# Sparse attention: the gate tiles go to one PSUM bank and the logits take turns in three

## The chip, the cores and the metric

The kernel runs on one core of a Trainium2 chip. The metric is the device time of one execution in microseconds (us); the time before is the median of three executions. The engines are called PE (TensorE), DVE (VectorE), ACT (ScalarE), POOL (GpSimd) and SP (SyncE).

## The reference

The program computes two blocks over 512 tokens of width 1024: a layer of gated linear attention and one of sparse attention, then a hybrid layer of five mixers. The change touches the sparse attention only:

```python
def dsa_mixer(x, cos_h, sin_h, cos_i, sin_i, w_in, w_out):
    ...
    h = x @ w_in                                  # q, k, v, z, indexer parts
    q = apply_partial_rope(h[..., :o1]...)        # 16 heads of 128
    k = apply_partial_rope(h[..., o1:o2]...)      # one key head, shared
    z = h[..., o3:o4]                             # the gate, 16 tiles of 128 columns
    ...
    logits = einsum('bthd,btjd->bthj', q_b, k_sel) * ATTN_SCALE
    probs = softmax(where(valid, logits, -inf))
    o = einsum('bthj,btjd->bthd', probs, v_sel)
    return (o * jax.nn.silu(z)) @ w_out
```

## The kernel before

Everything is written out by hand for each engine, with semaphores between them; there is no scheduler. `phase_dsa` computes the sparse attention feature-major: `qT` (the trace calls it mix_a) holds the queries of 16 heads, `zT` (mix_b) their gates, each head one tile of 128 features x 512 tokens. Selection is a mask: all causal logits are computed and `bias` (the tile `left` in the trace) takes the keys out that the indexer did not choose.

**Tiles.** A query or gate tile is 24 matmuls of 512 columns (8 slices of the width, three products each: high by high, high by low, low by high) into one PSUM bank. PE's `project(n)` makes tile n; tiles 0 to 15 are queries, 16 to 31 gates. Tiles 0 to 21 (`n_early` is 22) are made before the heads; tiles 22 to 31 are made in halves of 12 matmuls between the steps of the heads: both halves of tiles 22, 23, 24, 25 in heads 0, 1, 2, 3, and one half in each of heads 4 to 15 (tile 26 in heads 4 and 5, and so on). A gate tile is freed by two steps: ACT takes tanh of it into `zT` (L1505), DVE multiplies `zT` by the tile (L1592, semaphore `z_gated`). DVE does that for the tile finished in head h after the four masks of head h + 2 and a stream shuffle (L1560, heads 0 to 5 only).

**PSUM.** There are 8 banks. Banks 0 and 1 hold logits (`m % 2`, where m = 4 * head + block), 2 and 3 turned probabilities, 4 and 5 the head's output, 6 and 7 the tiles of `project` (`6 + n % 2`). So tile n waits until tile n - 2 is freed, and logits m wait until logits m - 2 are masked:

```python
if m >= 2:
    pe.wait_ge(sem["masked"], past["masked"] + m - 1)
n = (j + 1) * P
g.product(ps[:, m % 2, 0:n], qT[:, h, j * P:(j + 1) * P], kT[:, 0:n])
```

**One head on PE**, in this order: turn blocks 0 and 1 of the probabilities (L1438), half a gate tile, turn the output of the head before (L1444), turn blocks 2 and 3, in heads 0 to 3 the other half of a tile, `logits(h + 2)`, then the products of head h with v. `logits(h + 2)` is four products of 128, 256, 384 and 512 columns; each is two matmul records (the trace shows `ps<-dsa_kT,mix_a`). The product with v (`ps<-dsa_v,probT`) waits for the copies of the turned probabilities (ACT L1541, DVE L1651) and is 20 records.

**One head on DVE**: reciprocal, copy of block 1 of the turned probabilities (L1651), `gate_out` of the head before (L1664), copy of block 3 (L1651), `mask(h + 2)` (L1636: adds bias to the logits, takes the row's maximum in a second record, and L1639 scales it; the second record raises `masked`), the shuffle, the gate of a tile, and the output's scaling (L1657).

Of the kernel before, what the change touches and what calls it, by code (L numbers as in the profile page):

```python
# [14 lines left out]
P = 128  # L15
T = 512
NT = T // P
D = 1024
KD = D // P
# [15 lines left out]
class Semaphores(dict):  # L35
# [26 lines left out]
    def add(self, name, n):  # L62

        self.count[name] += n
        return n
# [193 lines left out]
def columns(parts, k, cols=slice(None)):  # L259

    return [part[:, k, cols] for part in parts]
# [1016 lines left out]
DSA_HEADS, DH, IDX_HEADS, IDX_DIM, TOPK = 16, 128, 8, 64, 128  # L1278
# [15 lines left out]
def phase_dsa(g, qT, zT, gT, first):  # L1294

    nc, t, ps = g.nc, g.t, g.ps
    sem, past, count, add = g.sem, g.sem.past, g.sem.count, g.sem.add
    IT = IDX_HEADS * IDX_DIM // P
    with ExitStack() as stack:
        kT = g.sb(stack, "dsa_kT", [P, T])  # L1300
# [6 lines left out]
        prob = g.sb(stack, "prob", [P, 2, NT, T])  # L1307
# [7 lines left out]
        bias = left  # L1315
# [7 lines left out]
        PER = CHUNK // P  # L1323
# [3 lines left out]
        n_scores = n_group + 3 * IDX_HEADS // n_group  # L1327
        n_silu = 4
        n_early = DSA_HEADS + n_silu + 2
        late_halves = [(n_early + i // 2, i % 2) for i in range(2 * (n_tiles - n_early))]  # L1330
        two_each = len(late_halves) - DSA_HEADS
        first_half = lambda h: 2 * min(h, two_each) + max(h - two_each, 0)
# [7 lines left out]
        if block:  # L1340

            @block.tensor
            def _(pe):
                w = g.chunk(pe, c_kv)
                tile_ready(pe, 1)
                for j in range(NT):
# [3 lines left out]
                    for k in range(KD):  # L1350
                        ins = g.split_product(ps[:, 1, j * DH:(j + 1) * DH], columns(g.xT, k, slice(j * P, (j + 1) * P)), columns(w, k, slice(DH, 2 * DH)), k == 0, k == KD - 1)
                ins.then_inc(sem["v_tok_ready"], add("v_tok_ready", 1))
                for k in range(KD):
                    ins = g.split_product(ps[:, 0, :], columns(w, k, slice(0, DH)), columns(g.xT, k), k == 0, k == KD - 1)
                ins.then_inc(sem["kT_ready"], add("kT_ready", 1))
                g.release("kT_ready")
                for i in range(IT):
                    if i % PER == 0:
                        w = g.chunk(pe, c_qi + i // PER)
                    for k in range(KD):  # L1360
                        ins = g.split_product(ps[:, 2 + i, :], columns(w, k, slice(i % PER * P, (i % PER + 1) * P)), columns(g.xT, k), k == 0, k == KD - 1)
# [3 lines left out]
                w = g.chunk(pe, c_ki)  # L1365
                for k in range(KD):
                    ins = g.split_product(ps[0:IDX_DIM + IDX_HEADS, 7, :], columns(w, k), columns(g.xT, k), k == 0, k == KD - 1)
# [5 lines left out]
                def project(n, ks=range(KD)):  # L1373

                    if n % PER == 0 and 0 in ks:
                        chunk[0] = g.chunk(pe, c_heads + n // PER)
                    w = chunk[0]
                    if 0 not in ks:
                        pass
                    elif n == 0:  # L1380
                        pass
                    elif n == 1:
                        pe.wait_ge(sem["wi_copied"], past["wi_copied"] + 1)
                    else:
                        b = n - 2
                        done = "q_copied" if b < DSA_HEADS else "z_gated"
                        pe.wait_ge(sem[done], past[done] + b % DSA_HEADS + 1)
                    for k in ks:
                        ins = g.split_product(ps[:, 6 + n % 2, :], columns(w, k, slice(n % PER * P, (n % PER + 1) * P)), columns(g.xT, k), k == 0, k == KD - 1)
                    if KD - 1 not in ks:  # L1390
                        return
                    ins.then_inc(sem["head_ready"], add("head_ready", 1))
                    if n % PER == PER - 1:
                        g.release("head_ready")

                project(0)
                pe.wait_ge(sem["wiT_copied"], past["wiT_copied"] + 1)
                pe.wait_ge(sem["kiT_ready"], past["kiT_ready"] + 2)
                for j in range(NT):
                    ins = nc.tensor.transpose(ps[:, 7, j * IDX_HEADS:(j + 1) * IDX_HEADS], wiT[:, j * P:(j + 1) * P], g.ident[0:IDX_HEADS, 0:IDX_HEADS])  # L1400
                ins.then_inc(sem["wi_ready"], add("wi_ready", 1))
                for n in range(1, 4):
                    project(n)
# [3 lines left out]
                for m, (j, h) in enumerate(pairs):  # L1407
# [3 lines left out]
                    n = (j + 1) * P  # L1411
# [6 lines left out]
                def logits(h):  # L1418
                    pe.wait_ge(sem["q_rotated"], past["q_rotated"] + h + 1)
                    if h == 0:  # L1420
                        pe.wait_ge(sem["kT_rotated"], past["kT_rotated"] + 1)
                        pe.wait_ge(sem["summed"], past["summed"] + len(pairs))
                    for j in range(NT):
                        m = NT * h + j
                        if m >= 2:
                            pe.wait_ge(sem["masked"], past["masked"] + m - 1)
                        n = (j + 1) * P
                        g.product(ps[:, m % 2, 0:n], qT[:, h, j * P:(j + 1) * P], kT[:, 0:n]).then_inc(sem["logits_ready"], add("logits_ready", 1))

                def turn_prob(h, j):  # L1430
                    m = NT * h + j
# [17 lines left out]
                for h in range(DSA_HEADS):  # L1449
# [16 lines left out]
                    for j in range(NT):  # L1466
                        for i in range(j + 1):
                            ins = g.product(ps[:, 4 + h % 2, j * P:(j + 1) * P], probT[:, i, j * P:(j + 1) * P], v[:, i, :], i == 0, i == j)
# [4 lines left out]
            def _(act):  # L1473
# [22 lines left out]
                def project(n):  # L1496
                    h = n % DSA_HEADS
                    act.wait_ge(sem["head_ready"], past["head_ready"] + n + 1)
                    src = ps[:, 6 + n % 2, :]
                    if n < DSA_HEADS:  # L1500
                        nc.scalar.activation(qT[:, h, :], src, ACT.Copy).then_inc(sem["q_copied"], add("q_copied", 1))
                    elif h < n_silu:
                        nc.scalar.activation(zT[:, h, :], src, ACT.Silu).then_inc(sem["z_gated"], add("z_gated", 1))
                    else:
                        nc.scalar.activation(zT[:, h, :], src, ACT.Tanh, scale=0.5).then_inc(sem["z_tanh"], add("z_tanh", 1))  # L1505
                    if n % PER == PER - 1:
                        g.split_high(act, c_heads + n // PER + 1 + RING)
# [3 lines left out]
                for m, (j, h) in enumerate(pairs):  # L1511
                    n = (j + 1) * P
# [22 lines left out]
                for h in range(DSA_HEADS):  # L1535
                    for j in range(0, NT, 2):
                        m = NT * h + j
# [14 lines left out]
            def _(dve):  # L1552
# [35 lines left out]
                def project(n):  # L1588

                    h = n - DSA_HEADS  # L1590
                    dve.wait_ge(sem["z_tanh"], past["z_tanh"] + h - n_silu + 1)
                    nc.vector.scalar_tensor_tensor(out=zT[:, h, :], in0=zT[:, h, :], scalar=1.0, in1=ps[:, 6 + n % 2, :],  # L1592
                                                   op0=ALU.add, op1=ALU.mult).then_inc(sem["z_gated"], add("z_gated", 1))

                for n in range(4):
# [2 lines left out]
                for m, (j, h) in enumerate(pairs):  # L1598
                    n = (j + 1) * P
                    dve.wait_ge(sem["relu"], past["relu"] + m + 1)  # L1600
                    r, w, s = ps[:, score_bank(m), 0:n], wi[:, j, h:h + 1], score[:, j, 0:n]
                    if h == 0:
                        ins = nc.vector.tensor_scalar(s, r, w, None, ALU.mult)
                    else:
                        dve.wait_ge(sem["summed"], past["summed"] + m)
                        ins = nc.vector.scalar_tensor_tensor(out=s, in0=r, scalar=w, in1=s, op0=ALU.mult, op1=ALU.add)
# [11 lines left out]
                for j in score_tiles:  # L1618
                    then(nc.vector.tensor_tensor(score[:, j, j * P:(j + 1) * P], score[:, j, j * P:(j + 1) * P], bias[:, 0, 0:P], ALU.add))
                    n = (j + 1) * P  # L1620
                    for r in range(TOPK // 8):
                        src = (left if r else score)[:, j, 0:n]
# [5 lines left out]
                def mask(h):  # L1628
                    for j in range(NT):
                        m = NT * h + j  # L1630
                        i = m % (2 * NT)
                        n = (j + 1) * P
                        dve.wait_ge(sem["logits_ready"], past["logits_ready"] + m + 1)
                        if h >= 2:
                            dve.wait_ge(sem["prob_turned"], past["prob_turned"] + m - 2 * NT + 1)
                        nc.vector.tensor_tensor_reduce(out=prob[:, h % 2, j, 0:n], in0=ps[:, m % 2, 0:n], in1=bias[:, j, 0:n],  # L1636
                                                                        scale=1.0, scalar=TAKEN, op0=ALU.add, op1=ALU.max, accum_out=peak[:, i:i + 1]).then_inc(sem["masked"], add("masked", 1))
                        dve.wait_ge(sem["masked"], past["masked"] + m + 1)
                        nc.vector.tensor_scalar(shift[:, i:i + 1], peak[:, i:i + 1], -ATTN_SCALE, None, ALU.mult).then_inc(sem["peak_shift"], add("peak_shift", 1))  # L1639
# [1801 lines left out]
def build(nc, t, out, upto=99, dump=None):  # L3441
    g = Program(nc, t, out)
    with g.ctx:
# [84 lines left out]
        with ExitStack() as stack:  # L3528
            mix_at = g.address()
            mix_a, mix_b = (g.sb(stack, f"mix_{n}", [P, KI, T]) for n in "ab")  # L3530

            gT = [g.alias(f"gT_{part}", [P, KI, T], F32R, mix_at + 4 * KI * T * i) for i, part in enumerate(("high", "low"))]
            if upto >= 1:
                phase_gla(g, mix_a, mix_b, gT, gla_first)
            if upto >= 2:
                phase_post(g, 0, gT, post_first[0], False, mix_at)
            if upto >= 3:
                phase_dsa(g, mix_a, mix_b, gT, dsa_first)
            if upto >= 4:
                phase_post(g, 1, gT, post_first[1], True, mix_at)  # L3540
# [30 lines left out]
```

## Time and profile before

| what | value |
|---|---|
| median of 3 executions | 1539.26 us (1538.21 to 1539.73) |
| the profiled execution | 1538.63 us |
| its span on the chip | 1536.7 us |
| PE busy | 1460.2 us, 95% |
| DVE / ACT / POOL busy | 637.6 / 523.9 / 554.4 us |
| mean granted clock of PE | 0.982 |
| heads of the sparse attention | 733 to 889 us from the span's start |

All times in the rows below are microseconds from the start of the span. The profiled execution spends 1.9 us outside its span. A busy PE is not PE at its peak: matmuls are pipelined, one starts long before the record of the one ahead of it ends, so the distance between two starts tells what a matmul costs, and the record's length does not.

### The profile page before, as it was taken

The numbers are of one execution on the slowest core, as the hardware profiler recorded it, in microseconds if no ns is written. First come the engines' busy times: TensorE is split into PE (matmuls) and PEld (weight loads), VectorE is DVE, ScalarE is ACT, GpSimd is POOL, SyncE is SP. The second block draws the span as 40 slices with busy tenths as digits, with TensorE's granted clock in tenths as the row PEclk, the third lists the DMA queues.
The fourth block names the chain that finished last, engine by engine and source line by source line (L and its number), as shares of the span: only waits on it lengthen the run. The fifth ranks groups of instructions, "written<-read, shape, count | busy, mean of one in ns | idle before, by whom it ended". The sixth has DMA issues, their size and how long they took to land. (4 is left out here: it accounts for less than half of the span.)

```text
span 1536.7 us, 25099 instructions
## 1 busy us (share of the span) xinstructions
PE 1460.2 (95%) x10829; PEld 1267.2 (82%) x10829; DVE 637.6 (41%) x1309; ACT 523.9 (34%) x862; POOL 554.4 (36%) x234
## 2 busy tenths in 40 slices
PE   7999999999999999999999999998999999877997
PEld 7898886899997987777777799888988887657886
DVE  6032441133117255389565511634125313576426
ACT  3355223433212322423544421335334224343310
POOL 6423421143332325963462243322434241062212
PEclk9999999999999999999999999999999999988999
DMA  5222220022531322223100053224332220002211
GB/s 169 83 83 83 82 83 28 28 85 86 200 99 67 108 65 88 77 85 108 56 28 29 28 185 104 83 65 148 83 110 84 81 83 28 1 1 74 86 39 55
DMA packets 113756, 121.31 MB, mean 79 GB/s; under 512 B 12529, under 2 KB 107613, under 8 KB 113390
## 3 DMA queue, kind: packets, MB, share of 16 engines
q1 hardware_dynamic: 110096, 113.77, 22.8%
q10 hardware_dynamic: 3550, 5.94, 1.1%
q8 instruction: 85, 1.39, 0.4%
q14 instruction: 25, 0.20, 0.0%
HBM read 113.41 MB, written 6.29 MB: 78 GB/s over the span
## 5 line engine op out<-in xcount | busy, mean ns | idle before, releaser
L196 POOL TENSOR_TENSOR w_low<-w_ring,w_high 128x2048 fp32r<-128x2048 f32 (+2 forms) x94 | 414.8, 4413 | 730.6 <-ACT w_high L184 730.4
L212 PE MATMUL ps<-w_high,xT_high 128*128 128x256 f32 (+1 forms) x1056 | 304.9, 289 | 9.4 <-POOL w_low L454 4.5
L212 PE MATMUL ps<-w_high,xT_low 128*128 128x256 f32 (+1 forms) x1056 | 299.3, 283 | 0.0
L212 PE MATMUL ps<-w_low,xT_high 128*128 128x256 f32 (+1 forms) x1056 | 299.1, 283 | 0.0
L184 ACT ACTIVATE w_high<-w_ring 128x2048 fp32r<-128x2048 f32 (+1 forms) x91 | 171.5, 1885 | 289.8 <-PE ps L212 285.8
L212 PE MATMUL ps<-xT_high,w_high 128*128 128x512 f32 (+1 forms) x600 | 241.2, 402 | 4.0 <-POOL w_low L196 3.0
L212 PE MATMUL ps<-xT_high,w_low 128*128 128x512 f32 (+1 forms) x600 | 238.3, 397 | 0.0
L212 PE MATMUL ps<-xT_low,w_high 128*128 128x512 f32 (+1 forms) x600 | 237.1, 395 | 0.0
L212 PEld LDWEIGHTS ps<-w_high,xT_high 128*128 128x128 f32 x1056 | 202.9, 192 | 17.1 <-issue 7.0
L212 PEld LDWEIGHTS ps<-w_low,xT_high 128*128 128x128 f32 x1056 | 202.8, 192 | 1.7 <-issue 1.7
L212 PEld LDWEIGHTS ps<-w_high,xT_low 128*128 128x128 f32 x1056 | 202.5, 192 | 0.0
L212 PE MATMUL ps<-w_high,gT_high 128*128 128x256 f32 x512 | 145.5, 284 | 3.9 <-DVE gT_low L291 3.9
L212 PE MATMUL ps<-w_high,gT_low 128*128 128x256 f32 x512 | 144.9, 283 | 0.0
L212 PE MATMUL ps<-w_low,gT_high 128*128 128x256 f32 x512 | 144.9, 283 | 0.0
L212 PEld LDWEIGHTS ps<-xT_high,w_high 128*128 128x128 f32 (+1 forms) x600 | 112.3, 187 | 34.2 <-POOL w_low L196 4.0
L212 PEld LDWEIGHTS ps<-xT_high,w_low 128*128 128x128 f32 (+1 forms) x600 | 112.3, 187 | 28.0
L212 PEld LDWEIGHTS ps<-xT_low,w_high 128*128 128x128 f32 (+1 forms) x600 | 112.5, 188 | 26.6
L212 PEld LDWEIGHTS ps<-w_high,gT_high 128*128 128x128 f32 x512 | 98.2, 192 | 4.4 <-DVE gT_low L291 4.4
L212 PEld LDWEIGHTS ps<-w_low,gT_high 128*128 128x128 f32 x512 | 98.3, 192 | 0.0
L212 PEld LDWEIGHTS ps<-w_high,gT_low 128*128 128x128 f32 x512 | 98.2, 192 | 0.0
L1170 DVE SCALAR_TENSOR_TENSOR x<-x,ps 128x512 f32<-128x512 f32 x16 | 10.9, 684 | 102.6 <-PE ps L212 102.6
L1700 POOL TENSOR_TENSOR gT_low<-dsa_gated,gT_high 128x512 fp32r<-128x512 f32 x16 | 20.7, 1294 | 84.7 <-ACT gT_high L1531 84.6
(505 smaller groups left out, 2187.6 us busy)
## 6 DMA issues: line engine op xcount, KB each, us to landing
w_ring<-in_gla_w_in_dram SPq DMA_DIRECT2D x24, 1024.0 KB, 5.3
w_ring<-in_dsa_w_in_dram SPq DMA_DIRECT2D x19, 1024.0 KB, 4.9
w_ring<-in_w_in_dram SPq DMA_DIRECT2D x18, 1024.0 KB, 5.1
w_ring<-in_gla_w_out_dram SPq DMA_DIRECT2D x8, 1024.0 KB, 5.2
w_ring<-in_ple_gate_w_dram SPq DMA_DIRECT2D x8, 1024.0 KB, 5.0
w_ring<-in_dsa_w_out_dram SPq DMA_DIRECT2D x8, 1024.0 KB, 5.1
x_scratch<-x SPq DMA_DIRECT2D x4, 1024.0 KB, 6.7
w_ring<-in_w_out_dram SPq DMA_DIRECT2D x4, 768.0 KB, 4.6
```

The costliest lines, as they stand in the source:

```text
L184: self.nc.scalar.activation(self.slot(self.w_high, i % RING, k, cols), self.slot(self.w_ring, n % RING, k, cols), ACT.Copy).then_inc(self. ...
L196: ins = self.nc.gpsimd.tensor_tensor(low[:, part], whole[:, part], high[:, part].bitcast(F32), ALU.subtract)
L212: return self.nc.tensor.matmul(out, lhs, rhs, start=first, stop=last, skip_group_check=not check)
L1170: nc.vector.scalar_tensor_tensor(out=r[:, j, cols], in0=x[:, j, cols], scalar=ALPHA, in1=ps[:, i, :], op0=ALU.mult, op1=ALU.add).then_inc( ...
L1700: nc.gpsimd.tensor_tensor(gT[1][:, h, :], gated[:, h % 2, :], gT[0][:, h, :].bitcast(F32), ALU.subtract).then_inc(sem["head_low"], add("he ...
```

## The change

The gate tiles from 22 on all use bank 6, so each of them but the first waits for the tile before it instead of the one before that. Bank 7, free after tile 21, becomes a third bank for the logits from head 2 on (m = 8): they go to banks 0, 1 and 7 in turn, and wait for the mask three products back instead of two. Logits m = 8 wait in addition until tile 21 is freed. No instruction is added, removed or moved on any engine: PE, DVE, ACT, POOL and SP execute the same rows in the same order, and what differs is the bank that some rows name and the value that some of PE's waits ask for.

```diff
+        tile_bank = lambda n: 6 + n % 2 if n < n_early else 6
+        third = 2 * NT
+        logit_bank = lambda m: (0, 1, 7)[m % 3] if m >= third else m % 2
...
                     else:
-                        b = n - 2
+                        b = n - 1 if n > n_early else n - 2
                         done = "q_copied" if b < DSA_HEADS else "z_gated"
                         pe.wait_ge(sem[done], past[done] + b % DSA_HEADS + 1)
                     for k in ks:
-                        ins = g.split_product(ps[:, 6 + n % 2, :], ...)
+                        ins = g.split_product(ps[:, tile_bank(n), :], ...)
...
                         m = NT * h + j
+                        if m == third:
+                            pe.wait_ge(sem["z_gated"], past["z_gated"] + n_early - DSA_HEADS)
                         if m >= 2:
-                            pe.wait_ge(sem["masked"], past["masked"] + m - 1)
+                            pe.wait_ge(sem["masked"], past["masked"] + (m - 2 if m > third else m - 1))
                         n = (j + 1) * P
-                        g.product(ps[:, m % 2, 0:n], ...)
+                        g.product(ps[:, logit_bank(m), 0:n], ...)
```

ACT's tanh and DVE's gate read `tile_bank(n)`, and DVE's mask reads `logit_bank(m)`.

## Rows read from the trace of the kernel before

**Rows 1.** Waits of all engines in 725 to 892: who waited for whom, total, times, longest.
```profile
PEld ps L212 <- DVE peak L1636: 15.1, 33, 0.7
```

**Rows 2.** Waits of PE in 725 to 892.
```profile
PE ps L212 <- DVE peak L1636: 4.1, 12, 0.4
PE ps L212 <- ACT probT L1541: 1.7, 2, 0.8
```

**Rows 3.** Busy time in stretches: nine heads, then two stretches after the attention.
```profile
784.37:868.28 83.91, 80.92 (x488) 65.04 (x487) 48.33 (x162) 39.81 (x106) 34.21 (x21) 1.00 0.12 39
...
1053.00:1060.00 7.00, 5.01 (x24) 4.92 (x25) 6.49 (x14) 4.97 (x14) 0.00 (x0) 0.51 0.40 150
...
1193.00:1197.00 4.00, 4.00 (x24) 4.00 (x23) 3.97 (x6) 0.00 (x0) 0.00 (x0) 0.57 0.17 60
```

**Rows 4.** Timeline of PE, logits(8) in head 6: start, length, tile, records.
```profile
803.02 0.28 PE L212 MATMUL ps<-dsa_kT,mix_a 128*128 128x128 f32 x1
803.24 0.60 PE L212 MATMUL ps<-dsa_kT,mix_a 128*128 128x256 f32 x2
804.17 0.59 PE L212 MATMUL ps<-dsa_kT,mix_a 128*128 128x384 f32 x1 [0.33 <-DVE peak L1636]
804.60 0.91 PE L212 MATMUL ps<-dsa_kT,mix_a 128*128 128x384 f32 x2
804.92 1.02 PE L212 MATMUL ps<-dsa_kT,mix_a 128*128 128x512 f32 x2
805.35 0.59 PE L212 MATMUL ps<-dsa_kT,mix_a 128*128 128x512 f32 x1
805.78 0.27 PE L212 MATMUL ps<-dsa_v,probT 128*128 128x128 f32 x1
```

**Rows 5.** Timeline of DVE around the same logits.
```profile
803.22 0.69 DVE L1651 COPY probT<-ps 128x512 f32<-128x512 f32 x1
803.83 0.28 DVE L1636 CUSTOM_DVE_ANT_0 prob<-ps,left 128x128 f32<-128x128 f32 x1
804.03 0.08 DVE L1636 DVE_READ_ACCUMULATOR2_ANT peak<- 128x1 f32 x1
```

**Rows 6.** Timeline of PE, logits(2) in head 0.
```profile
740.21 0.27 PE L212 MATMUL ps<-dsa_kT,mix_a 128*128 128x128 f32 x1
740.99 0.91 PE L212 MATMUL ps<-dsa_kT,mix_a 128*128 128x384 f32 x2
742.60 0.27 PE L212 MATMUL ps<-dsa_v,probT 128*128 128x128 f32 x1
```

**Rows 7.** Timeline: the gates of tiles 21 and 22, and PE's first weight load of tile 23.
```profile
734.53 0.68 DVE L1592 SCALAR_TENSOR_TENSOR mix_b<-mix_b,ps 128x512 f32<-128x512 f32 x1
740.41 0.60 ACT L1505 ACTIVATE mix_b<-ps 128x512 f32<-128x512 f32 x1 [2.75 <-PE ps L212]
744.28 0.66 DVE L1592 SCALAR_TENSOR_TENSOR mix_b<-mix_b,ps 128x512 f32<-128x512 f32 x1
745.05 0.19 PEld L212 LDWEIGHTS ps<-xT_high,w_high 128*128 128x128 f32 x1
```

**Rows 8.** Timeline: masks, shuffle and gate of tile 26 in head 5, load of tile 27.
```profile
795.79 0.56 DVE L1636 CUSTOM_DVE_ANT_0 prob<-ps,left 128x384 f32<-128x384 f32 x1 [0.23 <-PE ps L212]
796.65 0.69 DVE L1636 CUSTOM_DVE_ANT_0 prob<-ps,left 128x512 f32<-128x512 f32 x1
798.12 0.66 DVE L1592 SCALAR_TENSOR_TENSOR mix_b<-mix_b,ps 128x512 f32<-128x512 f32 x1
798.90 0.19 PEld L212 LDWEIGHTS ps<-xT_high,w_high 128*128 128x128 f32 x1
```

**Rows 9.** Timeline: gate of tile 27 in head 7, load of tile 28.
```profile
816.11 0.68 DVE L1592 SCALAR_TENSOR_TENSOR mix_b<-mix_b,ps 128x512 f32<-128x512 f32 x1
817.55 0.19 PEld L212 LDWEIGHTS ps<-xT_high,w_high 128*128 128x128 f32 x1
```

More of the change, by code:

```diff
@@ L1388, in project @@
                     for k in ks:
-                        ins = g.split_product(ps[:, 6 + n % 2, :], columns(w, k, slice(n % PER * P, (n % PER + 1) * P)), columns(g.xT, k), k == 0, k == KD - 1)
+                        ins = g.split_product(ps[:, tile_bank(n), :], columns(w, k, slice(n % PER * P, (n % PER + 1) * P)), columns(g.xT, k), k == 0, k == KD - 1)
                     if KD - 1 not in ks:
@@ L1424, in logits @@
                         m = NT * h + j
+                        if m == third:
+                            pe.wait_ge(sem["z_gated"], past["z_gated"] + n_early - DSA_HEADS)
                         if m >= 2:
-                            pe.wait_ge(sem["masked"], past["masked"] + m - 1)
+                            pe.wait_ge(sem["masked"], past["masked"] + (m - 2 if m > third else m - 1))
                         n = (j + 1) * P
-                        g.product(ps[:, m % 2, 0:n], qT[:, h, j * P:(j + 1) * P], kT[:, 0:n]).then_inc(sem["logits_ready"], add("logits_ready", 1))
+                        g.product(ps[:, logit_bank(m), 0:n], qT[:, h, j * P:(j + 1) * P], kT[:, 0:n]).then_inc(sem["logits_ready"], add("logits_ready", 1))
                 def turn_prob(h, j):
@@ L1498, in project @@
                     act.wait_ge(sem["head_ready"], past["head_ready"] + n + 1)
-                    src = ps[:, 6 + n % 2, :]
+                    src = ps[:, tile_bank(n), :]
                     if n < DSA_HEADS:
@@ L1591, in project @@
                     dve.wait_ge(sem["z_tanh"], past["z_tanh"] + h - n_silu + 1)
-                    nc.vector.scalar_tensor_tensor(out=zT[:, h, :], in0=zT[:, h, :], scalar=1.0, in1=ps[:, 6 + n % 2, :],
+                    nc.vector.scalar_tensor_tensor(out=zT[:, h, :], in0=zT[:, h, :], scalar=1.0, in1=ps[:, tile_bank(n), :],
                                                    op0=ALU.add, op1=ALU.mult).then_inc(sem["z_gated"], add("z_gated", 1))
@@ L1635, in mask @@
                             dve.wait_ge(sem["prob_turned"], past["prob_turned"] + m - 2 * NT + 1)
-                        nc.vector.tensor_tensor_reduce(out=prob[:, h % 2, j, 0:n], in0=ps[:, m % 2, 0:n], in1=bias[:, j, 0:n],
+                        nc.vector.tensor_tensor_reduce(out=prob[:, h % 2, j, 0:n], in0=ps[:, logit_bank(m), 0:n], in1=bias[:, j, 0:n],
                                                                         scale=1.0, scalar=TAKEN, op0=ALU.add, op1=ALU.max, accum_out=peak[:, i:i + 1]).then_inc(sem["masked"], add("masked", 1))
```

## The prediction

> **What bounds the kernel now.** I read first who waits for whom in the stage that is touched, then the stage's busy times, then the timeline of one head. In 725 to 892 the records of PE show 4.1 us of idle time before products of L212 that the masks of L1636 release, in 12 places, and 1.7 us for the copies of the turned probabilities [rows 2]. The weight loads ahead of the same products wait 15.1 us in 33 places for the same masks [rows 1]. So PE waits for the logits' banks, and the question is how long. From 784.37 (logits(6)) to 868.28 (logits(15)) lie nine heads, 9.32 us each; PE is busy 80.92 of 83.91 us, DVE only 48.33, 5.4 us a head, and ACT 39.81 [rows 3]. PE sets the pace of this stage, at full granted clock (1.00), and a microsecond taken from its wait is a microsecond of the program as long as nothing takes the wait's place.
>
> The timeline of logits(8) shows the wait [rows 4]. The products start at 803.02 (128 columns), 803.24 (256), 804.17 (384) and 804.92 (512), and the product with v at 805.78: 2.76 us. What they would need without a wait comes from starts that nothing holds up: two records of 128 columns from 803.02 to 803.24, 0.11 us each; 256 columns, twice that, 0.22; 384 columns from 804.60 to 804.92, 0.32; 512 columns from 804.92 to 805.35, 0.43. Twice each is 2.16 us. The difference is **0.60 us**: 384 columns could have started at 803.68 (803.24 + 0.44) and started at 804.17, and their first record kept the array 0.43 instead of 0.32, since the weights for the second weren't loaded ahead. The 512 columns lose nothing: 804.60 + 0.32 is 804.92.
>
> Why it waits: bank m % 2 of the third block is that of the first block, and DVE's mask of that starts at 803.83, when the copy of the turned block (803.22, 0.69 long) is nearly through; the maximum is out at 804.11, and PE goes on at 804.17, 0.06 later [rows 4, 5]. In heads 0 to 3 a half tile lies between the turns and the logits, so the copy is long done; there the same stretch is 740.21 to 742.60, 2.39 us, and 0.23 are lost [rows 6].
>
> **The change, part by part.** *Third bank for the logits.* 14 heads (0 to 13) make logits with m of 8 or more. The third block now waits for a mask of the head before, long done, and the fourth for the first block's mask. In the ten heads 4 to 13 that mask releases at 804.17 in the times of [rows 4], where the fourth block's weights would be wanted at 803.68 + 0.32 = 804.00 and its first column at 804.32; a load needs the 0.11 by which loads and starts of 128 columns follow each other, so 804.28 is in time. Gain: 10 x 0.60 = 6.0 us. In heads 0 to 3 it is 4 x 0.23 = 0.9 us. Together 6.9 us. Next in PE's queue is the product with v, which waits for DVE's copy: it ends at 803.91 and the product comes to 805.18, 1.2 us to spare [rows 4, 5]. Heads 14 and 15 have no logits in between, and the 1.7 us there [rows 2] stay.
>
> *The extra wait of m = 8* for tile 21: its gate ends at 735.21, logits(2) start at 740.21 [rows 6, 7]. Cost 0; without this cover it would hold PE with everything behind it in its queue.
>
> *One bank for the gates.* Nine tiles (23 to 31) now wait for the tile just before. What stands behind this wait on PE is the half tile, the turns of blocks 2 and 3, and with them DVE's copies and ACT's. The release is DVE's gate, queued behind four masks and a shuffle. Tile 22's is through at 744.94, 0.06 more for the release, and PE wants the weights of tile 23 at 745.05: 0.05 us to spare [rows 7]. Both ends come 0.23 earlier after the change, since in these heads the masks of blocks 3 and 4 wait for PE's logits themselves; so tile 23 is a tie, and tiles 24 to 26, whose gates and loads repeat this pattern, are too; I take 0.1 us for the four together. Tile 27 (made from head 6 on) is not quite: PE wants it at 798.90 now and 0.60 earlier, 798.30, then. DVE gains less: the 0.23 that block 3's mask idled, and 0.14 since the mask of 384 columns takes 0.56 + 0.16 (the 0.16 is what lies beyond the record between 803.83 and 804.27, 0.44 for a mask of 0.28) where 0.86 went by from 795.79 to 796.65. So the gate ends at 798.78 - 0.37 = 798.41 and releases at 798.47: **0.17 us late** [rows 5, 8]. Tiles 28 to 31 have no shuffle before them: the gate is through at 816.79 now, 816.42 then, and wanted at 817.55 - 0.60 = 816.95 [rows 9]. Cost of this part 0.1 + 0.17, about 0.3 us; the bound from above, if each of the nine came late by a whole mask of 0.69 [rows 8], is 6.2 us.
>
> The DMAs, POOL's work and everything behind the attention are released by these engines, and come earlier by the same time.
>
> **Sum.** 6.9 - 0.3 = 6.6 us. The profiled execution, 1538.63 us with a span of 1536.7, would take 1532.0; the median of the three is 0.63 above it, so I predict 1539.26 - 6.6 = **1532.7 us**. The lower bound of the gain is what the records show as idle. With 4.1 us, less the waits of logits(0) and (1), which stay, it is about ten times the 0.33 of [rows 4], 3.3 us, less 0.3: 1536.3. I take the distances between starts, because the records of 256 columns run to 803.84 (803.24 + 0.60), 0.16 us after the next start could have come at 803.68 [rows 4], so idle between records misses that much at each wait.
>
> On this choice the Trainium skill ("Perfetto Trace Analysis", Identifying the Most-Contended Engine) has a rule: matmul busy time is a bad measure, since matmuls are pipelined. By the busy time the sum is 3.0 us of gain, by the starts 6.6.
>
> **Rivals.** *A: the gates bind.* A single bank makes each tile's start wait for its predecessor's whole evacuation. For it: five of nine starts have no more than 0.05 us to spare. Against it: between two tiles lie the logits, v and two turns, and the gate is through in that time. If DVE is one mask (0.69) later than I reckon at the five tight starts, 3.5 us are lost and 3.1 are left: 1536.2. Chance 0.08. *A as a loss, the other side:* with evacuation fully exposed, ACT 0.60 and DVE 0.66 [rows 7], nine starts cost 11.3 us, and the program ends 4.4 slower, 1543.7. It decides against the change from 0.77 us per start (6.9 / 9) and shows as slower than the bound below from 1.1. Chance 0.03.
>
> The Trainium skill says as much ("Perfetto Trace Analysis", Matmuls): independent matmul groups should rotate through banks, so that one's evacuation overlaps the next's matmuls. It speaks for the logits' part and against the gates'; in the trace the next gate tile does not follow at once, so I give it little.
>
> *B: the wait only moves.* If the first block's mask came later after the change, the fourth block would wait in place of the third. For it: that mask follows the copy of a block that PE has just turned. Against it: that copy's time hangs on PE alone, and DVE has 9.32 - 5.4 us of slack a head. The idle records alone would then be won, 3.0: 1536.3. Chance 0.07. *C: the granted clock elsewhere.* The stages after come earlier by 6.6 us and may meet the low clock otherwise: in 1193 to 1197 PE worked all the 4.0 us at 0.57, which cost 1.7 [rows 3]. One such stretch more or less is 1.7 us, two 3.4. This widens the range both ways and is no case of its own, but at a chance of 0.03 it takes 4 us or more of the gain.
>
> **Chances and range.** My forecast 0.79, A 0.08, B 0.07, C 0.03, A as a loss 0.03. A measurement of this kernel tells about 0.2%, 3.1 us, from no change. Faster by more (under 1536.2): my forecast and half of A, B and C, 0.88. Within it: 0.09. Slower by more: 0.03. The range: below, the full 6.9 and one stretch of low clock less, 1530.7; above, where A and B lie, 1536.3.
>
> **What would show it.** In the profile after: the waits of PE's products for L1636 fall from 4.1 us to the 0.7 of the first two heads or so; heads 4 to 13 take 8.72 us instead of 9.32, with 2.16 from the first logits to the product with v; a new wait of PE for L1592 is seen at tile 27, under 0.2 us, and perhaps at 23 to 26; PE's copies and DVE's order stay. I am wrong if PE waits for L1592 at nine tiles by 0.7 us or more each, if the wait for L1636 stands before the fourth block with 0.5 us, or if the heads gain 6 us and the stages after 1053 give them back.

## The result, and the profile after

| | before | after |
|---|---|---|
| median of six executions each, taken in turns | 1538.85 us | 1531.0 us (1528.66 to 1532.64) |
| ratio, 95% interval | | 0.9947 (0.9936 to 0.9959) |
| profiled execution, span | 1538.63, 1536.7 us | 1532.64, 1530.9 us |
| the kernel again, five executions (run e1) | 1538.18 us | 1531.74 us, ratio 0.9954 (0.9942 to 0.9965) |

By the ratio the kernel is faster by 0.53%, 8.2 us of 1538.85, on the first measurement and by 0.46%, 7.1 us, on the second; the first pair of medians differs by 7.85 us, the second by 6.44. Forecast were 6.6 us. The page of the kernel after, its first two lines:

```profile
span 1530.9 us, 25099 instructions
...
PE 1458.2 (95%) x10829; PEld 1269.7 (83%) x10829; DVE 636.9 (42%) x1309; ACT 522.6 (34%) x862; POOL 554.2 (36%) x234
```

The waits of PE in 725 to 892, kernel after; it answers to [rows 2] (the lines of the file moved by 5, so L1641 is the mask that was L1636):

```profile
PE ps L212 <- ACT probT L1546: 1.7, 2, 0.8
PE ps L1449 <- DVE kiT L1662: 0.8, 1, 0.8
PE ps L212 <- DVE peak L1641: 0.7, 2, 0.4
```

Of the twelve waits for the masks two are left, those of the first two heads. The weight loads of PE still wait for the masks in 15 places, 5.3 us in all instead of 15.1 [rows 1], but that costs nothing, as the timeline of logits(8) shows. First PE, then its weight loads, then DVE; start, length, tile, records:

```profile
801.80 0.28 PE L212 MATMUL ps<-dsa_kT,mix_a 128*128 128x128 f32 x1
...
802.46 0.81 PE L212 MATMUL ps<-dsa_kT,mix_a 128*128 128x384 f32 x2
802.78 0.91 PE L212 MATMUL ps<-dsa_kT,mix_a 128*128 128x384 f32 x2
803.10 1.02 PE L212 MATMUL ps<-dsa_kT,mix_a 128*128 128x512 f32 x2
803.53 0.59 PE L212 MATMUL ps<-dsa_kT,mix_a 128*128 128x512 f32 x1
803.96 0.27 PE L212 MATMUL ps<-dsa_v,probT 128*128 128x128 f32 x1
...
802.95 0.34 PEld L212 LDWEIGHTS ps<-dsa_kT,mix_a 128*128 128x128 f32 x2 [0.30 <-DVE peak L1641]
...
802.00 0.69 DVE L1656 COPY probT<-ps 128x512 f32<-128x512 f32 x1
802.61 0.28 DVE L1641 CUSTOM_DVE_ANT_0 prob<-ps,left 128x128 f32<-128x128 f32 x1
802.82 0.08 DVE L1641 DVE_READ_ACCUMULATOR2_ANT peak<- 128x1 f32 x1
```

From 801.80 to 803.96 lie 2.16 us, where 2.76 lay in [rows 4]. The 384 columns start 0.66 after the first product, and both their records take 0.32. The load that waits is now that of the fourth block: it is let go at 802.95, 0.05 after the maximum of the first block is out (802.82 + 0.08), and the 512 columns start at 803.10, the 0.32 after 802.78 that they would have needed anyway. The wait is there and costs nothing.

Busy time of nine heads, logits(6) to logits(15), kernel after (PE, PEld, DVE, ACT, POOL, granted clock, DMA share, GB/s):

```profile
784.21:862.84 78.63, 78.63 (x488) 65.70 (x487) 47.59 (x162) 38.79 (x106) 34.41 (x21) 1.00 0.12 41
```

It answers to the first of [rows 3]: 8.74 us a head instead of 9.32, and PE has no idle time left.

The gates: DVE's gate of tile 22 and the first load of tile 23, then the gate of tile 26 in head 5, PE's turn and the load of tile 27 (timeline, kernel after), for [rows 7, 8]:

```profile
744.79 0.66 DVE L1597 SCALAR_TENSOR_TENSOR mix_b<-mix_b,ps 128x512 f32<-128x512 f32 x1
...
745.56 0.19 PEld L212 LDWEIGHTS ps<-xT_high,w_high 128*128 128x128 f32 x1
...
796.99 0.66 DVE L1597 SCALAR_TENSOR_TENSOR mix_b<-mix_b,ps 128x512 f32<-128x512 f32 x1
...
797.34 0.49 PE L1443 MATMUL ps<-ident,prob 128*128 128x128 f32 x3
...
797.70 0.19 PEld L212 LDWEIGHTS ps<-xT_high,w_high 128*128 128x128 f32 x1
```

Tile 23 is loaded 0.11 after the gate ends, as before the change: no wait. Tile 27 is loaded at 797.70, 0.05 after its gate, and its matmuls start 0.36 after the turn where the other heads show 0.25: 0.11 us lost.

Last, the whole attention, from the first product of logits(2) to the first of the output projection, and what comes behind it. Kernel before, then kernel after:

```profile
740.21:889.90 149.69, 143.93 (x863) 116.57 (x862) 82.82 (x266) 68.30 (x172) 60.26 (x38) 1.00 0.09 29
889.90:1536.70 646.80, 598.84 (x5467) 534.53 (x5465) 257.39 (x506) 207.50 (x342) 200.27 (x73) 0.97 0.24 78
```
```profile
740.95:883.85 142.90, 140.46 (x863) 117.72 (x862) 82.00 (x266) 67.16 (x172) 60.20 (x38) 1.00 0.09 30
883.85:1530.90 647.05, 599.04 (x5467) 534.71 (x5465) 257.33 (x506) 207.46 (x342) 200.29 (x73) 0.97 0.24 78
```

The attention is 6.79 us shorter (149.69 - 142.90). The part ahead of it took 0.74 us more in this execution and the part behind 0.25 more, so the spans differ by 5.8. The medians differ by 7.85. What lies between these three numbers is the question that the experiments had to answer.

### The profile page after: what moved, and what is told of

Read it like the earlier page. It is cut to its first block and busy times, and to the rows that moved or that the text cites. A ratio compares the mean times of both kernels' runs of the same rounds, so it can differ in the third digit from the quotient of the medians.

```text
span 1530.9 us, 25099 instructions
## 1 busy us (share of the span) xinstructions
PE 1458.2 (95%) x10829; PEld 1269.7 (83%) x10829; DVE 636.9 (42%) x1309; ACT 522.6 (34%) x862; POOL 554.2 (36%) x234
## 5 line engine op out<-in xcount | busy, mean ns | idle before, releaser
L196 POOL TENSOR_TENSOR w_low<-w_ring,w_high 128x2048 fp32r<-128x2048 f32 (+2 forms) x94 | 414.8, 4414 | 731.8 <-ACT w_high L184 731.6
L212 PE MATMUL ps<-w_high,mix_high 128*128 128x256 f32 (+1 forms) x144 | 45.3, 315 | 6.3 <-DVE late L3313 3.9
```

The lines of the kernel that those rows point to most:

```text
L196: ins = self.nc.gpsimd.tensor_tensor(low[:, part], whole[:, part], high[:, part].bitcast(F32), ALU.subtract)
L212: return self.nc.tensor.matmul(out, lhs, rhs, start=first, stop=last, skip_group_check=not check)
```

## The experiments

**Theory.** The change takes 6.8 us out of the attention, in every execution, by the wait for the masks alone; the rest of the difference is low granted clock elsewhere (the clock of PE that the profile shows as granted, 1.00 for full), which moves from execution to execution. **Rivals.** The change gains 8 us, a part outside the attention; the banks and not the waits make the gain; a single bank for the gates costs much that something else pays for.

### The same two kernels again (e1, e2)

No edit: the kernel after, and the kernel before.

> The changed kernel itself once more, to see what varies. Theory: the attention gains 6.8 us by the trace (first logits of head 0 to the last turn), always; what the median gained beyond that, 8.2 us in all against 6.6 forecast, is the low granted clock before and behind the attention, which falls in other places and lengths from execution to execution. Then the new ratio lies nearer 0.9956 (6.8 us) than 0.9947, single runs spread over 3 us or more again, and the profile shows the attention's length equal to that of the first profile within 0.1 us while the stretches of low clock outside it differ. Rival: the change gains 8 us in every execution, 1.4 of it outside the attention; then the ratio is 0.9947 again and the parts outside the attention are shorter than before by 1.4 us at like clock.

> The kernel before once more, nothing changed: what no change looks like. Ratio 1.000 within 0.1%; the attention as long as in the first profile of before within 0.1 us. If single runs differ by 3 us here too, the spread is not the change's. By the theory the stretches of low clock outside the attention move; by the rival (a gain of 8 us in every execution) they stay.

Measured: e1 1531.74 us, ratio 0.9954 (0.9942 to 0.9965), single executions 1529.52 to 1533.01; e2 1538.71 us, ratio 1.0001 (0.9993 to 1.001), single executions 1536.03 to 1540.33. The kernel before spreads over 4 us as well. Windows of e2, attention and behind:

```profile
741.83:891.65 149.82, 144.03 (x863) 116.59 (x862) 82.76 (x266) 68.27 (x172) 60.19 (x38) 1.00 0.09 29
891.65:1536.10 644.45, 600.37 (x5467) 535.09 (x5465) 257.57 (x506) 207.72 (x342) 200.55 (x73) 0.97 0.24 78
```

The same program, and behind the attention it took 644.45 us where the first profile has 646.80; the attention is the same within 0.13. The part that the change doesn't touch varies by 2.4 us between these two executions of one kernel. The ratio of e1 lies at the 0.9956 that 6.8 us would give, and the part behind the attention (647.05 us in the first profile of the kernel after, 646.79 in e1) is within 0.3 us of the first profile of before and longer than in e2, so the rival that 1.4 us are gained there every time finds no support. The two ratios themselves can't tell 6.8 us from 8: their intervals overlap.

### One half of the change, and its banks without its wait (e3, e4)

e3 keeps the gates' single bank and takes the third bank for the logits back; e4 keeps both edits of the banks, but lets PE wait for the mask two products back again:

```diff
 # e3
-        logit_bank = lambda m: (0, 1, 7)[m % 3] if m >= third else m % 2
+        logit_bank = lambda m: m % 2
 # e3 and e4
-                            pe.wait_ge(sem["masked"], past["masked"] + (m - 2 if m > third else m - 1))
+                            pe.wait_ge(sem["masked"], past["masked"] + m - 1)
```

> Half of the change: the gate tiles from 22 on in bank 6 alone, the logits in banks 0 and 1 as before (bank 7 idle, the extra wait for tile 21 kept). Theory: in the old pace every gate is released 0.05 us before PE wants the next tile's weights, so this costs 0 to 0.3 us: ratio 1.000, no or hardly any wait of PE for L1592, waits for the masks 4.1 us as before. Rival (a single bank exposes the evacuation at each of nine starts): a wait at each, 3 us or more, ratio 1.002 or above.

> The change with the logits in three banks, but waiting for the mask two products back as before. Nothing is left out of the computation. Theory: the gain is the wait's alone, so it vanishes: the waits for the masks are 4.1 us again, the heads take 9.32 us, ratio 1.000. Rival (other banks are faster in themselves, by less interference of DVE's reads and PE's writes): a part of the gain stays, at least 1 us.

Measured: e3 1538.35 us, ratio 1.0 (0.9992 to 1.0009); e4 1538.94 us, ratio 1.0001 (0.9992 to 1.0011). Both show 4.1 us in 12 waits of PE for the masks. The attention by the same marks (first e3, then e4) is as long as the 149.69 and 149.82 us of the kernel before, and so are nine heads of e4, logits(6) to logits(15):

```profile
741.80:891.57 149.77, 143.99 (x863) 116.60 (x862) 82.76 (x266) 68.28 (x172) 60.21 (x38) 1.00 0.09 29
```
```profile
742.05:891.79 149.74, 143.96 (x863) 116.59 (x862) 82.76 (x266) 68.28 (x172) 60.14 (x38) 1.00 0.09 29
...
786.19:870.12 83.93, 80.93 (x488) 65.05 (x487) 48.29 (x162) 39.81 (x106) 34.20 (x21) 1.00 0.12 39
```

So a single bank for the gates costs nothing in the old pace, and three banks gain nothing as long as PE waits for the same mask: the gain is the wait's.

### How near the single bank is to its edge (e5, e6)

DVE's gate of a tile goes behind `scale_out`, which waits for the product with v: in e5 on the kernel after (one bank), in e6 on the kernel before (two). The last `gate_out` then waits for the last gate.

```diff
-                    for n in late_done(h):
-                        project(n)
                     scale_out(h)
+                    for n in late_done(h):
+                        project(n)
...
+                dve.wait_ge(sem["z_gated"], past["z_gated"] + DSA_HEADS)
                 gate_out(DSA_HEADS - 1)
```

> The changed kernel with DVE's gate of a tile put behind the scaling of the head's output, which waits for the product with v. Theory: with one bank each of the nine tile starts waits for that gate. The scaling starts about when PE has ended the product, 0.20 us after the first turn; 0.69 for it, 0.66 for the gate and 0.06 for the release make the gate 1.3 to 1.4 us later than PE wants the weights: 9 x 1.36 = 12.2 us more than the changed kernel, 5.4 more than before, ratio 1.0035. Rival (the single bank has slack that I do not see): under 5 us more than the changed kernel, ratio under 0.999.

> The kernel before, two banks for the tiles, with the same late gate. Theory: a tile waits for the tile two before it, so the late gate costs nothing: ratio 1.000, no wait of PE for L1592, waits for the masks 4.1 us. Rival: the late gate is itself the cost (it pushes back DVE's next copy, which PE's turns wait for), and then this kernel is slower too, by 3 us or more.

Measured: e5 1545.27 us, ratio 1.0046 (1.0032 to 1.0059); e6 1538.58 us, ratio 0.9994 (0.9983 to 1.0004), with 4.0 us of waits for the masks and none for a gate. PE's waits in e5, and one of the nine starts (tile 28 in head 8), timeline:

```profile
PE ps L212 <- DVE mix_b L1597: 9.8, 9, 1.1
...
821.70 0.69 DVE L1662 TENSOR_TENSOR kiT<-ps,inv_total 128x512 f32<-128x512 f32 x1 [1.14 <-PE ps L212]
822.31 0.68 DVE L1597 SCALAR_TENSOR_TENSOR mix_b<-mix_b,ps 128x512 f32<-128x512 f32 x1
...
823.13 0.47 PE L212 MATMUL ps<-xT_high,w_high 128*128 128x512 f32 x1 [1.14 <-DVE mix_b L1597]
```

The gate ends at 822.99, and PE starts the tile at 823.13, after a turn at 821.50: 1.63 us, where 0.25 is usual. The attention takes 154.9 us by the same marks, 12.0 more than with the gate in its place, 1.33 for each of the nine starts; 12.2 were expected. With one bank the late gate costs 12 us, and with two banks nothing (the attention of e6 takes 149.68 us). So a single bank can cost more than the third bank gains, once its release comes late; in the kernel after, the gate is just early enough.

### The waits that are left (e7, e8)

In heads 14 and 15 no logits cover the copies of the turned probabilities, and PE waits 1.7 us for ACT [rows 2]. In e7 the half tile of these heads is cut in two: a quarter tile stays before `turn_out`, the other quarter goes behind the turns of blocks 2 and 3, where it covers the copies. DVE's gate goes ahead of the shuffle. e8 also lets POOL make the low half of head 15 before the split of the weights.

```diff
                     for n, half in halves_of(h)[:1]:
-                        project(n, half_tiles[half])
+                        ks = half_tiles[half]
+                        project(n, ks[:2] if last_two else ks)
                     if h:
                         turn_out(h - 1)
                     turn_prob(h, 2)
                     turn_prob(h, 3)
+                    for n, half in halves_of(h)[:1]:
+                        if last_two:
+                            project(n, half_tiles[half][2:])
...
-                    if n_scores + h < DSA_HEADS:
-                        swap_query(n_scores + h)
                     for n in late_done(h):
                         project(n)
+                    if n_scores + h < DSA_HEADS:
+                        swap_query(n_scores + h)
```

> The changed kernel, improved in two places: the gate ahead of the shuffle (frees tile 26 in time for tile 27, 0.11 us), and in heads 14 and 15, which have no logits to cover the copies of the turned probabilities, only a quarter of the half tile before the turn of blocks 2 and 3 and the rest behind it. Theory: the two waits of PE for L1541, 0.83 us each in the records and about 1.0 from start to start, go: the attention takes 140.8 us instead of 142.9 and the program 2 us less, ratio 0.994. Rival: tile 31 is ready later, ACT's and POOL's splits of the next weights start later, and POOL's low half of head 15, behind them, holds PE at the start of the output projection: the attention is shorter, the stage after it longer, and little or nothing of the 2 us stays.

> As the one before, and POOL makes the low half of head 15 ahead of the split of the weights. Theory: if the rival of the run before holds, this one gives the 2 us back: PE does not wait for POOL at the start of the output projection, ratio 0.994. Rival: the split of the weights then comes too late for PE at the second chunk of the projection, with a wait for L196 of up to 4.6 us.

Measured: e7 1529.68 us, ratio 0.9942 (0.9928 to 0.9955); e8 1529.51 us, ratio 0.9942 (0.993 to 0.9955). The attention of e7, and the end of head 14 on PE, where the quarter tile runs from the turns to the product with v without a gap:

```profile
741.39:882.00 140.61, 139.83 (x863) 117.64 (x862) 82.08 (x266) 67.28 (x172) 59.08 (x37) 1.00 0.09 31
...
869.69 0.93 PE L1443 MATMUL ps<-ident,prob 128*128 128x128 f32 x7
870.37 0.48 PE L212 MATMUL ps<-xT_high,w_high 128*128 128x512 f32 x1
...
871.63 0.39 PE L212 MATMUL ps<-xT_high,w_low 128*128 128x512 f32 x1
871.86 2.39 PE L212 MATMUL ps<-dsa_v,probT 128*128 128x128 f32 x20
```

140.61 us are 2.29 less than with the change alone, of which 0.11 is tile 27's start. Up to 960 no wait of PE for POOL appears in e7, and the one behind that, 1.7 us for `w_low` of L196, stands in the kernel after as well. The part behind the attention takes 645.9 us in e7 and in e8, within what the kernel after shows (643.3 to 647.2, below). So the rival of e7 fell, and with it the reason for e8: both take the same time. Both beat the kernel before. That e7 also beats the kernel after is shown only by the length of the attention; the intervals of the times (around 0.9942, and around 0.9954 for e1) overlap.

### Four more executions of the kernel after (e9 to e12)

> The changed kernel, one execution with its profile; four such looks. Its single times fell into two groups, 1528.7 to 1529.7 and 1531.6 to 1533.0, and both profiles so far are of the upper one. Theory: the attention is 142.9 us within 0.1 in every look, and an execution of the lower group differs by one or two stretches of low granted clock fewer outside it, 1.7 us each where PE is busy throughout, as about 1190. Rival: in the lower group the attention itself, or a wait that the bank change took away elsewhere, is shorter by 2 us or more.

> As the look before: attention 142.9 us within 0.1, and what differs lies in the low clock outside it (theory), or in the attention (rival).

> As the looks before: attention 142.9 us within 0.1, and what differs lies in the low clock outside it (theory), or in the attention (rival).

> As the looks before: attention 142.9 us within 0.1, and what differs lies in the low clock outside it (theory), or in the attention (rival).

Measured, 1532.0, 1528.27, 1534.03 and 1528.11 us. The windows of e10 (the attention, behind it), then of e11:

```profile
740.27:883.18 142.91, 140.47 (x863) 117.72 (x862) 82.01 (x266) 67.19 (x172) 60.19 (x38) 1.00 0.09 30
883.18:1526.50 643.32, 596.71 (x5467) 532.77 (x5465) 257.66 (x506) 207.85 (x342) 200.44 (x73) 0.97 0.24 78
```
```profile
742.23:885.11 142.88, 140.44 (x863) 117.70 (x862) 81.98 (x266) 67.17 (x172) 60.15 (x38) 1.00 0.09 30
885.11:1532.30 647.19, 599.19 (x5467) 534.86 (x5465) 257.36 (x506) 207.39 (x342) 200.23 (x73) 0.97 0.24 78
```

One kernel, 5.8 us apart, and the attention is equal to 0.03 us: 2.0 us of the difference lie ahead of it (742.23 against 740.27) and 3.9 behind. One place where they arise, 1188 to 1192, in e10 and then in e11:

```profile
1188.00:1192.00 4.00, 4.00 (x36) 3.85 (x35) 3.06 (x7) 1.43 (x1) 0.00 (x0) 1.00 0.02 4
```
```profile
1188.00:1192.00 4.00, 4.00 (x23) 4.00 (x23) 3.99 (x5) 0.00 (x0) 0.00 (x0) 0.57 0.34 118
```

PE is busy throughout in both, but has 36 matmuls at a granted clock of 1.00 and 23 at 0.57, mostly the lower of its two levels, 1.2 GHz: 4.0 x 0.43 = 1.7 us of work less in the same time. These windows are equal in time, not in work. From one matmul to the same later one (it starts at 1193.10 in e10 and at 1197.81 in e11) the stretch takes 8.86 and 10.42 us, 1.56 more; a second such place, at 593, costs 1.55:

```profile
1184.24:1193.10 8.86, 8.86 (x76) 8.64 (x77) 6.82 (x11) 2.52 (x2) 0.54 (x1) 1.00 0.23 80
593.18:598.97 5.79, 5.79 (x24) 4.42 (x24) 5.68 (x6) 1.83 (x2) 3.88 (x1) 1.00 0.57 181
```
```profile
1187.39:1197.81 10.42, 10.42 (x75) 10.20 (x76) 6.82 (x11) 2.49 (x2) 0.51 (x1) 0.84 0.20 69
593.60:600.94 7.34, 7.34 (x24) 5.55 (x24) 7.23 (x6) 1.82 (x2) 5.14 (x1) 0.77 0.45 143
```

All six profiles of the kernel after, from the same marks:

| run | time | ahead of the attention | attention | behind |
|---|---|---|---|---|
| after | 1532.64 | 740.95 | 142.90 | 647.05 |
| e1 | 1533.01 | 741.63 | 142.88 | 646.79 |
| e9 | 1532.0 | 740.71 | 142.91 | 646.68 |
| e10 | 1528.27 | 740.27 | 142.91 | 643.32 |
| e11 | 1534.03 | 742.23 | 142.88 | 647.19 |
| e12 | 1528.11 | 740.17 | 142.87 | 643.36 |

The theory holds in all six: the attention is the same within 0.04 us, and the times that differ do so outside it. In the windows of 4 us around 1188, the granted clock is low in after, e9 and e11 and 1.00 in e1, e10 and e12. So that place alone doesn't make an execution long: e1 runs through it at 1.00 and still takes 646.79 us behind the attention. It is behind e10 elsewhere, by 2.2 us in this stretch, again between the same matmuls (e10, then e1):

```profile
1324.92:1371.93 47.01, 34.80 (x202) 25.07 (x203) 36.64 (x67) 23.67 (x65) 24.08 (x23) 0.85 0.00 1
```
```profile
1326.75:1375.94 49.19, 40.29 (x201) 27.79 (x202) 36.51 (x67) 23.59 (x65) 23.90 (x23) 0.72 0.00 1
```

The kernels whose attention is as long as before (before, e2, e3, e4 and e6) show the same spread behind it: 646.80, 644.45, 643.13, 647.11 and 646.82 us.

## Why the prediction was right, and where it was not

**What bounds the stage, and the wait:** right. The distance between starts was the measure to take: 0.60 us a head by the starts and 0.33 by the idle records [rows 4] gave 6.6 and 3.0 us, and 6.79 were gained. The Trainium skill ("Perfetto Trace Analysis", Identifying the Most-Contended Engine) says that matmul busy time is not a good measure of how close a kernel is to roofline. That is a rule about roofline and not about waits, but the trace shows busy time misleading here too: PE's busy time fell by 143.93 - 140.46 = 3.47 us only, while the stage became 6.79 shorter.

**The third bank, 6.9 us:** right. The starts of logits(8) were forecast at 2.16 us to the product with v and are there; the load of the fourth block was expected to be let go in time, and is.

**One bank for the gates, 0.3 us:** right in kind, a little too high. Tiles 23 to 26, put at 0.1 for the four, cost nothing; tile 27, put at 0.17 late, is 0.11 late. 6.9 - 0.11 = 6.8 is the attention's gain. The prediction gave the exposed evacuation (rival A as a loss) 0.03 and a price of 11.3 us, nine times ACT's 0.60 and DVE's 0.66. The 12.0 us of e5 are near it by coincidence: there PE waits for the output's scaling and the gate behind it, 1.33 us a start, and no run exposes ACT's part.

The Trainium skill's rule that independent matmul groups should rotate through banks ("Perfetto Trace Analysis", Matmuls) held for the logits (6.8 us). For the gates it would have been a wrong guide in the order of this kernel, where e3 shows no cost of the single bank, and it holds with the late gate: 12.0 us in e5 with one bank, nothing in e6 with two.

**B, the wait only moves:** the prediction was right to give it little. The wait of the loads did move to the fourth block, with 0.30 us at logits(8), and costs nothing.

**C and the range: this is the step that failed.** The prediction said that low clock elsewhere "widens the range both ways" and took for its lower end "the full 6.9 and one stretch of low clock less, 1530.7". Two terms of that bound were off: the spread, put at one stretch, and to a lesser part the base. One stretch is too few. The six profiles of the changed kernel show the parts outside the attention differing by 2.1 us ahead of it (742.23 - 740.17) and by 3.9 behind (647.19 - 643.32), more than two stretches of 1.7, and single executions from 1528.11 to 1534.03. Of the six executions of the first measurement three lay under 1530, below the range. Their median, 1531.0, is 0.3 us above its lower end, and 0.9947 of 1538.85 is 1530.69, at the very edge.

From the forecast of 1532.7 to the 1531.0 measured are 1.7 us. 0.4 of them are the base: the forecast started from the median of three executions, 1539.26, and that of six is 1538.85. 0.2 are the attention, 6.79 instead of 6.6. The other 1.1 are the medians' difference of 7.85 beyond the attention's 6.79, for which the sum had no term. The attention's gain is the same in all six profiles. That the 1.1 us are chance, from how many of the six executions came out short, is argued and not shown: over all fifteen executions of the kernel after on record and all 62 of the kernel before, the medians are 1531.74 and 1538.6 us, 6.9 apart, but the means differ by 7.5 (95% interval 6.5 to 8.5), so a further gain of up to 1.7 us outside the attention is not excluded. The term for the spread was mis-sized, at 1.7 where the runs show about twice that; the sum of the stage was not.

Whether the earlier start of the later stages changes how often they meet the low clock stays open: the place at 1188 in the kernel after, at 1193 to 1199 with the old attention, is low in three of six profiles of the kernel after and in three of the five with the old attention (before, e4, e6; not in e2 and e3). These counts show no change, and are too small to exclude one.

## What to carry to other kernels

A buffer that is short in one place can be taken from one that is long in another: ask of each user when its release comes and when it is wanted, from the order on the releasing engine, and give the bank to the one whose release is late. A wait of a pipelined engine is measured from start to start on either side of it, not by the idle time between records, which showed half of it here. And a forecast of a single stage should be tested on the length of that stage in the trace: here it is the same to 0.04 us in six executions whose whole times differ by 5.9.

## What the runs showed that was not expected

Two kinds of executions of one kernel with nothing between: 1528.1 to 1529.7 and 1531.6 to 1534.0 for the kernel after, and the two profiled executions of the lower kind have 3.3 to 3.9 us less behind the attention than the four others. The executions of the kernel before, 1535.0 to 1541.0, show no such gap, so with fifteen executions it may be chance. The places that were followed up to a number are 1188, 1.6 us with PE busy all the time, 593, also 1.6, and for e1 the stretch from 1327 to 1376, 2.2 us. All four profiles of the upper kind lose those 1.6 us at 593, and neither of the lower kind does; behind the attention after, e9 and e11 lose time at 1188, and e1 instead between 1327 and 1376. Why an execution meets the low clock in one of these places or not stays open.
